# One transformer step with split products: token chunks 364/364/360 against 128 plain and 2 x 480 split

## The reference

```python
h = rms_norm(x, g0) * (1 + sc_a) + sh_a
proj = h @ w_in                       # 1024 -> 2432, then attention and the RWKV-7 scan
m = concatenate([o_attn, o_rw]) @ w_out
x = x + gt_a * rms_norm(m, g1)
h = rms_norm(x, g2) * (1 + sc_f) + sh_f
f = (silu(h @ w_gate) * (h @ w_up)) @ w_down     # 1024 -> 2816 -> 1024
x = x + gt_f * rms_norm(f, g3)
```

## Time and profile before

| | |
|---|---|
| Median of 3 runs | 2487.2 us (2483.46 to 2495.3) |
| The profiled execution | span 2496.6 us, 9.4 us above the median |
| TensorE matmul busy | 2098.6 us, 84% |
| VectorE busy | 940.9 us, 38% |
| ScalarE busy | 642.4 us, 26% |
| GpSimd busy | 202.4 us, 8% |
| DMA | 147.53 MB, 59 GB/s in the mean |

### The profile page before, as it was taken

The page is one execution under the profiler, slowest core; times in us unless marked ns, Lnnn a source line. Parts: engine busy times, 40 slices in busy tenths (PEclk is TensorE's granted clock), DMA queues, the critical chain, the costliest instruction groups (busy, mean ns, idle before and its releaser), DMA issues. The chain is left out here.

```text
span 2496.6 us, 38394 instructions
## 1 busy us (share of the span) xinstructions
PE 2098.6 (84%) x15782; PEld 1779.0 (71%) x15782; DVE 940.9 (38%) x1433; ACT 642.4 (26%) x1215; POOL 202.4 (8%) x283
## 2 busy tenths in 40 slices
PE   7499974199889889879867598499999999999985
PEld 2499952066667657656652297399999999999984
DVE  2211154445344434434521803623422333323336
ACT  2523342023323323323421412521111111111101
POOL 0000000032323212312300000100000000000000
PEclk9799996599999978989978799799999999999998
DMA  6011115701001001000019231211111011111022
GB/s 241 29 47 42 34 51 149 195 27 41 17 20 38 16 17 41 16 16 18 4 42 293 73 117 41 73 35 51 51 51 43 18 42 50 50 45 40 19 98 72
DMA packets 112112, 147.53 MB, mean 59 GB/s; under 512 B 65920, under 2 KB 80896, under 8 KB 111520
## 3 DMA queue, kind: packets, MB, share of 16 engines
q1 hardware_dynamic: 111968, 145.41, 18.0%
HBM read 114.90 MB, written 30.50 MB: 58 GB/s over the span
## 5 line engine op out<-in xcount | busy, mean ns | idle before, releaser
L1848 PE MATMUL ps<-hhi,whi 128*128 128x364 f32 (+1 forms) x1056 | 348.5, 330 | 33.1 <-DVE hlo L1087 27.9
L1848 PE MATMUL ps<-hlo,whi 128*128 128x364 f32 (+1 forms) x1056 | 348.4, 330 | 0.0
L1848 PE MATMUL ps<-hhi,wlo 128*128 128x364 f32 (+1 forms) x1056 | 348.3, 330 | 0.0
L347 DVE TENSOR_TENSOR wlo<-wraw,whi 128x1024 fp32r<-128x1024 f32 x72 | 88.0, 1225 | 525.3 <-ACT whi L343 525.3
L360 PE MATMUL ps<-hhi,whi 128*128 128x364 f32 (+1 forms) x672 | 222.7, 331 | 58.6 <-DVE hlo L1087 31.8
L1848 PEld LDWEIGHTS ps<-hhi,whi 128*128 128x128 f32 x1056 | 199.7, 189 | 34.2 <-DVE hlo L1087 28.5
L360 PE MATMUL ps<-hlo,whi 128*128 128x364 f32 (+1 forms) x672 | 222.5, 331 | 0.0
L360 PE MATMUL ps<-hhi,wlo 128*128 128x364 f32 (+1 forms) x672 | 222.3, 331 | 0.0
L1825 PE MATMUL ps<-ahi,dhi 128*128 128x364 f32 x528 | 180.8, 342 | 24.9 <-DVE acc L1427 16.8
L1848 PEld LDWEIGHTS ps<-hlo,whi 128*128 128x128 f32 x1056 | 199.6, 189 | 0.0
L1848 PEld LDWEIGHTS ps<-hhi,wlo 128*128 128x128 f32 x1056 | 199.6, 189 | 0.0
(11 more groups left out here) (204 smaller groups left out, 3133.1 us busy)
## 6 DMA issues: line engine op xcount, KB each, us to landing
wraw<-in_w_tiles SPq DMA_DIRECT2D x72, 512.0 KB, 3.4
late<-in_ada_w SPq DMA_DIRECT2D x8, 2048.0 KB, 8.1
ci<-scan SPq DMA_DIRECT2D x17, 768.0 KB, 4.5
draw<-in_w_down SPq DMA_DIRECT2D x22, 512.0 KB, 3.3
slab<-in_ada_w SPq DMA_DIRECT2D x4, 2048.0 KB, 18.2
scan<-mix SPq DMA_DIRECT2D x12, 512.0 KB, 4.4
x<-in_x_t SPq DMA_DIRECT2D x4, 1456.0 KB, 9.6
x<-x_mid SPq DMA_DIRECT2D x1, 4352.0 KB, 14.1
```

The costliest lines, as they stand in the source:

```text
L347: nc.vector.tensor_tensor(wlo[u][:, :, :], wraw[u][:, :, :], whi[u][:, :, :].bitcast(F32), ALU.subtract).then_inc(w_lo, 1)
L1848: mm = nc.tensor.matmul(ps[:, 3 * u + c, 0:n], w[u][:, k, :], x[:, k, a:a + n], start=(k == 0 and w is whi and x is hhi), stop=(k == KD - ...
```

## The change

CH becomes (960, 128), (0, 480), (480, 480). Chunk 0 (WHOLE) is multiplied in plain fp32 straight from unsplit operands: the loaded weights wraw, and hf, a copy of the input's last 128 tokens. Chunks 1 and 2 stay split. In the down pass chunk 0 multiplies draw by af, and draw has two buffers, loaded as a pair once the preceding down pass has ended. A weight load now also waits until the plain part of that buffer's last tile is done. The attention's q and k chunks keep 364/364/360 (QCH). All norms, residuals and stores that loop over CH take the new chunks. In the diff, renamed semaphore counts in GpSimd's, ScalarE's and VectorE's other waits are left out.

```diff
@@ -44,7 +44,10 @@
 NEG = -1e30
-CH = [(0, 364), (364, 364), (728, 360)]
+TF = 960
+CH = [(TF, T - TF), (0, 480), (480, 480)]
+WHOLE = 0
+QCH = [(0, 364), (364, 364), (728, 360)]
 CM = 363
...
@@ -161,11 +164,13 @@
         wraw, whi, wlo = [wraw0, wraw1], [whi0, whi1], [wlo0, wlo1]
-        hhi, hlo, R2 = place(R1, ("hhi", [P, KD, T], F32R), ("hlo", [P, KD, T], F32R))
+        hhi, hlo, hf, end = place(R1, ("hhi", [P, KD, TF], F32R), ("hlo", [P, KD, TF], F32R), ("hf", [P, KD, T - TF]))
+        R2 = R1 + 2 * KD * T * 4
+        assert end <= R2
         END = nc.sbuf_usable_end
-        sq = [P, 4, 364]
+        sq = [P, 4, 480]
         x1, s0, s1, r0, r1, end = place(R2, ("x1", [P, KD, T]), ("sq1_0", sq), ("sq1_1", sq), ("mrow0", [2, 512]), ("mrow1", [2, 512]))
@@ -230,11 +235,11 @@
         assert end <= END
-            R2, ("acc", [P, KD, T]), ("ahi", [P, 4, T], F32R), ("alo", [P, 4, T], F32R), ("draw", [P, D]),
+            R2, ("acc", [P, KD, T]), ("ahi", [P, 4, TF], F32R), ("alo", [P, 4, TF], F32R), ("af", [P, 4, T - TF]), ("draw0", [P, D]), ("draw1", [P, D]),
         assert end <= END
...
@@ -326,13 +331,14 @@
         def o_parts(h):
-            return [(h[:, 0:KR, :], oatt[:, :, :]), (h[:, KR:KD, :], yt[:, :, :])]
+            return [(h[:, 0:KR, :], oatt[:, :, 0:TF]), (h[:, KR:KD, :], yt[:, :, 0:TF])]
         def load_weight(eng, m, u, first=False):
                 eng.wait_ge(w_lo, 2 * m + u - 1)
+                eng.wait_ge(out_ready[u], 3 * m - 2)
             eng.dma_start(wraw[u][:, :, :].rearrange("p a b -> p (a b)"), d["w_tiles"][2 * m + u, :, :]).then_inc(w_in_sem[u], 16)
@@ -348,18 +354,31 @@
         def project(pe, m, u, first=False, tokens=None):
-            pe.wait_ge(w_lo, 2 * m + u + 1)
-            for c, (a, n) in enumerate(CH):
-                if tokens is not None:
-                    pe.wait_ge(lo_ready, tokens + c + 1)
+            for c in range(3):
+                if c == WHOLE:
+                    pe.wait_ge(w_in_sem[u], 16 * (m + 1))
+                    if tokens is not None:
+                        pe.wait_ge(hf_ready, tokens // 2 + 1)
+                else:
+                    pe.wait_ge(w_lo, 2 * m + u + 1)
+                    if tokens is not None:
+                        pe.wait_ge(lo_ready, tokens + c)
                 if not first:
                     pe.wait_ge(bank_free[u], 3 * (m - 1) + c + 1)
-                out = ps[:, 3 * u + c, 0:n]
-                for k in range(KD):
+                tile_products(u, c).then_inc(out_ready[u], 1)
+
+        def tile_products(u, c):
+
+            a, n = CH[c]
+            out = ps[:, 3 * u + c, 0:n]
+            for k in range(KD):
+                if c == WHOLE:
+                    mm = nc.tensor.matmul(out, wraw[u][:, k, :], hf[:, k, :], start=(k == 0), stop=(k == KD - 1))
+                else:
                     for w, x in ((whi, hhi), (whi, hlo), (wlo, hhi)):
                                               start=(k == 0 and w is whi and x is hhi), stop=(k == KD - 1 and w is wlo))
-                mm.then_inc(out_ready[u], 1)
+            return mm
         NORMS = {"n1": (KD, D), "q": (KQ, QL), "kv": (KKV, KVL), "m": (KD, D), "n2": (KD, D), "f": (KD, D)}
@@ -575,6 +594,7 @@
             sp.wait_ge(osplit_lo, 2)
+            sp.wait_ge(hf_ready, 2)
             for c, (a, n) in enumerate(CH):
@@ -587,21 +607,27 @@
             sp.wait_ge(sq_used, first_piece["n2"] + 6)
-            def load_down(g, u, first=False):
+            def load_down(g, first=False):
                 if not first:
-                    sp.wait_ge(d_lo, 2 * g + u)
-                sp.dma_start(draw[:, :], d["w_down"][bass.ds((2 * g + u) * P, P), :]).then_inc(d_in, 16)
+                    sp.wait_ge(d_lo, 2 * g)
+                    sp.wait_ge(down_ready, 24 * g + 1)
+                for u in range(2):
+                    sp.dma_start(draw[u][:, :], d["w_down"][bass.ds((2 * g + u) * P, P), :]).then_inc(d_in[u], 16)
             load_weight(sp, FF_M + 1, 0)
             load_weight(sp, FF_M + 1, 1)
-            load_down(0, 0, first=True)
-            with sp.Fori(1, GROUPS) as g:
-                for j in range(2):
-                    for u in range(2):
-                        load_weight(sp, 2 * g + FF_M + j, u)
-                load_down(g - 1, 1)
-                load_down(g, 0)
-            load_down(GROUPS - 1, 1)
+            load_down(0, first=True)
+            load_weight(sp, FF_M + 2, 0)
+            load_weight(sp, FF_M + 2, 1)
+            load_weight(sp, FF_M + 3, 0)
+            load_weight(sp, FF_M + 3, 1)
+            with sp.Fori(2, GROUPS) as g:
+                for u in range(2):
+                    load_weight(sp, 2 * g + FF_M, u)
+                load_down(g - 1)
+                for u in range(2):
+                    load_weight(sp, 2 * g + FF_M + 1, u)
+            load_down(GROUPS - 1)
             for u in range(2):
...
@@ -717,12 +744,17 @@
                 a, n = CH[c]
-                for k in range(KD):
-                    for b, w, s in segments(c):
-                        step.mark(nc.scalar.activation(src[:, k, b:b + w], src[:, k, b:b + w], ACT.Identity,
-                                                       bias=mod[:, shift + k, s:s + 1], scale=gains[:, gain, k, s:s + 1]))
-                step.wait()
-                nc.scalar.copy(hhi[:, :, a:a + n], src[:, :, a:a + n]).then_inc(hi_ready, 1)
+                parts = [(k, b, w, s) for k in range(KD) for b, w, s in segments(c)]
+                for i, (k, b, w, s) in enumerate(parts):
+                    dst = hf[:, k, b - TF:b - TF + w] if c == WHOLE else src[:, k, b:b + w]
+                    ins = nc.scalar.activation(dst, src[:, k, b:b + w], ACT.Identity, bias=mod[:, shift + k, s:s + 1], scale=gains[:, gain, k, s:s + 1])
+                    if c == WHOLE and i == len(parts) - 1:
+                        ins.then_inc(hf_ready, 1)
+                    else:
+                        step.mark(ins)
+                if c != WHOLE:
+                    step.wait()
+                    nc.scalar.copy(hhi[:, :, a:a + n], src[:, :, a:a + n]).then_inc(hi_ready, 1)
             act.wait_ge(gains_done, 1)
...
@@ -995,11 +1028,16 @@
             act.wait_ge(mod_done, SLABS)
-            for dst, src in o_parts(hhi):
+            for i, (dst, src) in enumerate(o_parts(hhi)):
                 nc.scalar.copy(dst, src).then_inc(osplit_hi, 1)
+                ins = nc.scalar.copy(hf[:, KR * i:KR * i + KR, :], (oatt, yt)[i][:, :, TF:T])
+                if i == 0:
+                    step.mark(ins)
+            ins.then_inc(hf_ready, 1)
             act.wait_ge(osplit_lo, 2)
+            act.wait_ge(hf_ready, 2)
             for n in range(KD):
@@ -1019,24 +1057,28 @@
             def down_hi(g, u):
-                act.wait_ge(d_in, 16 * (2 * g + u + 1))
+                act.wait_ge(d_in[u], 16 * (g + 1))
                 act.wait_ge(down_ready, 24 * g + 1)
-                nc.scalar.copy(dhi[u][:, :], draw[:, :]).then_inc(d_hi, 1)
+                nc.scalar.copy(dhi[u][:, :], draw[u][:, :]).then_inc(d_hi, 1)
             def gate(g, slot, j, first=False, last=False):
                 m = 2 * g + FF_M + j
-                q = 6 * g + 3 * j
+                q, q2 = 6 * g + 3 * j, 4 * g + 2 * j
                 for c, (a, n) in enumerate(CH):
                     if not (first and j == 0):
-                        act.wait_ge(act_lo, q + c - 2)
+                        if c == WHOLE:
+                            act.wait_ge(prod_ready, q - 2)
+                        else:
+                            act.wait_ge(act_lo, q2 + c - 2)
                     nc.scalar.activation(sil[c][:, 0:n], ps[:, c, 0:n], ACT.Silu).then_inc(sil_ready, 1)
                     act.wait_ge(down_ready, 24 * (g - 1) + 1)
-                for c, (a, n) in enumerate(CH):
+                for c in (1, 2):
+                    a, n = CH[c]
                     act.wait_ge(prod_ready, q + c + 1)
@@ -1083,7 +1125,7 @@
                 a, n = CH[c]
-                dve.wait_ge(hi_ready, count + 1)
+                dve.wait_ge(hi_ready, count)
                 nc.vector.tensor_tensor(hlo[:, :, a:a + n], src[:, :, a:a + n], hhi[:, :, a:a + n].bitcast(F32), ALU.subtract).then_inc(lo_ready, 1)
...
@@ -1395,26 +1437,30 @@
                 times_rstd(m1, x2, c)
-            for c in range(3):
-                rest(m1, c, 3 + c)
+            for c in (1, 2):
+                rest(m1, c, 2 + c)
             def down_lo(g, u):
                 dve.wait_ge(d_hi, 2 * g + u + 1)
-                nc.vector.tensor_tensor(dlo[u][:, :], draw[:, :], dhi[u][:, :].bitcast(F32), ALU.subtract).then_inc(d_lo, 1)
-
-            def product(g, slot, j, last=False):
+                nc.vector.tensor_tensor(dlo[u][:, :], draw[u][:, :], dhi[u][:, :].bitcast(F32), ALU.subtract).then_inc(d_lo, 1)
+
+            def product(g, slot, j, first=False, last=False):
                 m = 2 * g + FF_M + j
```

(73 more changed lines are left out.)

12 lines of the change are left out of this document (6 added, 6 removed).

## The result

The changed kernel takes 2532.8 us (median of 4 runs, 2525.06 to 2535.72); the kernel before took 2485.33 us beside it (4 runs, 2481.48 to 2495.3). The ratio is 1.0184, with a 95% interval of 1.0155 to 1.0213. So it is slower by 1.8%, 47.5 us, and 21 us above the top of the forecast range. The forecast was 2480 us; rival (d), a fixed cost of every fp32r product, gave 2535 us.

A forecast was written before the change was run, and what follows sets the result against it. The kernel was taken as bound by how fast TensorE starts products where weight tiles are streamed. Terms -32.0 + 28.6 - 3.6 = -7.0 us gave 2489.6 us profiled, 2480 us as median, range 2452 to 2512 us.

The forecast's parts named there:

- rival (d): Every fp32r product: the 0.0148 us above 0.152 us is a fixed cost; +55 us, 2535 us; chance 0.08.
- What a product costs: TensorE's fp32r products: starts are paced by a floor of 0.1665 us, so 480 columns cost 0.2025 us.
- Weight tiles: 72 streamed input, output and gate/up tiles: each saves 0.42 us, 30.2 us together; -32.0 us with the first tile's start.
- the change of form: Weight tiles: 0.06 us added per tile for two switches between plain and split products, bounds 0 and 0.2.
- Down passes: 11 feed-forward down passes: adder waits lengthen them, ten passes take 300.0 us, the last 28.4 us; together +28.6 us.
- The hold: Down passes: TensorE waits 0.45 us for the adder and restarts 0.10 us late, 0.56 us, seven times a pass.
- The start of a pass: Down passes: the adder comes after splits and remainders; TensorE resumes at 3.94 us, its wait grows to 2.3 us.
- The rest: Small terms at start, output product, norms, last store and last down loads: sum -3.6 us, bounds within 3 us each.
- What was costed at nothing: Weight loads waiting for the previous tile's plain part, paired down loads queued behind the preceding pass: no cost expected.
- (b): Down passes: the clock falls in seven short idle gaps a pass, 27 us in 11 passes, 2507 us; chance 0.20.
- (c): Down passes: the adder doesn't hold TensorE, 11 x 3.9 us less, 2437 us; chance 0.08.
- (e): Tiles and down passes: plain records are held to 0.1665 us like fp32r, about 2546 us; chance 0.04.

The follow-up runs named there:

- the streams: Two kernels with only back-to-back products by width, form, weight columns and start column, not the step; 480 fp32r columns took 0.2167 and 0.2175 us.
- the third experiment: Changed kernel with the 16 wide units of each down pass first and the 8 plain ones after: 2496.84 us, ratio 1.0046 to the kernel before.
- the first stream kernel: Computes nothing of the step, only streams of 96 products differing in width, form, weight columns and start column; 480 fp32r columns took 0.2167 us.
- the sixth experiment: Changed kernel with wide down units first and VectorE's remainders and weight split between the first additions: 2482.02 us, ratio 0.9994 to the kernel before.
- run 48: Not a follow-up run: "run" is the verb here, groups of four tiles run 48 products in 10.48 or 10.32 us; no measured kernel time belongs to it.

## Why the prediction was wrong

**The step that failed** is the one under "What a product costs": "So something else paces them, a floor of 0.1665 us", and from it "I take 0.2025 us" for 480 columns. It rested on two readings. The first, 360 columns no quicker than 364, was within the scatter of start columns (3 ns, where four columns are 1.7 ns). The second, no extra at half clock, is a sound row, but it doesn't exclude what I took it to exclude: the extra of about 0.015 us is there at 364 and at 480 columns alike and yet goes away at 1.2 GHz, as the after trace shows with 0.400 us for 480. Measured were 0.215 to 0.217 us for 480 columns, in the changed kernel and alone. Two points so close together can't tell a floor from a fixed cost, and I gave the fixed cost, rival (d), only 0.08.

**Weight tiles.** Forecast 11.56 us, measured 12.10 us. 48 products at 0.215 instead of 0.2025 us are +0.60 us; the 0.06 us for the change of form isn't there (10.32 + 1.78 us leaves nothing between), and 16 records at 0.1114 us are 1.78 us, as forecast. 72 x 0.54 = 39 us of the miss are here. The deeper mistake is the same one: with a fixed cost for each product, going from three chunks to two saves 24 x 0.015 = 0.36 us a tile, and the plain chunk costs 1.78 - 1.28 = 0.5 us more than its columns would in wide chunks. If part of the extra grows with the columns, as the streams suggest, both figures are smaller and their difference, 0.12 to 0.14 us, stays.

**Down passes.** The hold was forecast with its place, size and number: seven a pass of 0.56 us, "some 88 times, 40 to 60 us in total", and there were 85, 41.6 us, with the late restart on top. The start of a pass was right as well (wait 2.3 us forecast; the longest is 2.1). Summed over the chain, the ten passes took 306.5 us against 300.0 forecast, and the last one 31.5 against 28.4 us. The stretches of the first, second and fifth pass (columns as in the earlier trace rows; the granted clock is the third figure from the right):

```profile
1707.30:1739.00 31.70, 27.86 (x130) 23.20 (x130) 14.50 (x27) 1.54 (x2) 0.00 (x0) 0.95 0.00 1
1787.50:1818.00 30.50, 26.34 (x130) 22.00 (x129) 14.39 (x27) 1.54 (x2) 0.00 (x0) 1.00 0.00 1
...
2024.40:2056.00 31.60, 27.75 (x129) 23.17 (x128) 14.48 (x27) 1.54 (x2) 0.00 (x0) 0.95 0.00 0
```

At full clock the forecast was 29.3 us, and 96 wide products at 0.0135 us more make 30.6 us, which is what seven passes took. Two of the ten had a stretch at half clock, +1.1 us each, where I had counted 0.7 us for every pass; the tenth, with no weight split before it, took 29.1 us. The last pass is 1.3 us of the same and 1.8 us at its start: its first 6.0 us are at half clock, which costs 3.0 us where I had counted 1.5. One term of before was off too: the ten old passes took 270.4 us in the chain, not 273.4, since the tenth took 24.6 us. An addition of 480 columns, forecast at 0.65 us, took 0.65 to 0.67; the 3.19 us behind that forecast are VectorE's longest piece at L1087 (2912 columns), a row that the earlier trace rows doesn't show.

**The rest.** The small terms came to about what was forecast: the feed-forward part starts 1.6 us earlier (1607.7 against 1609.3 us), though the input tiles end 2.5 us later (338.1 against 335.6 us). What was costed at nothing did cost nothing: no wait for a weight load shows among TensorE's waits, and for the down loads only that before the last pass, 7.5 us where it was 8.1.

**Sum.** 39 us of tiles, 6.5 and 3.1 us of passes make 48.6 us; 2489.6 us was forecast for the profiled execution and its span was 2533.6 us, 44 us more, so some 5 us were better elsewhere. The forecast had taken over the old span with its two waits of 2.5 us behind down passes and the half clock behind one of them, 5.1 + 1.8 = 6.9 us; the changed kernel has neither, and no term of the forecast stood for that. The other 9 us of the miss of 52.8 us are the distance that I took over between execution and median; the profiled execution after lies 0.8 us above its median in span, and that before lay 9.4 us above.

**The rivals.** (b), a clock that falls in the idle gaps within a pass, didn't happen. The Trainium skill, "TensorE: Matmul & The Clock Gate", A second HAM failure mode, would have idling between groups of products, while PSUM banks are cycled through, make the clock swing. Here seven holds of about half a microsecond in each pass went by with the granted clock at 1.00, the level of 2.4 GHz; it fell in two of the ten, each time within 2 us behind the wait of 2 us at the start. (c) fell with the waits, (e) with the plain pace of 0.1115 us. (d) came true for 480 columns, in kind and in amount (that the extra isn't quite fixed in narrower products changes nothing here): it added 55 us, and by the measured paces it is 39 us in the tiles and 96 x 11 x 0.0135 = 14 us in the passes, 53 us. That its total of 2535 us lies so near to 2532.8 us is partly luck, since the offset between execution and median (+9 us) was made up by the clock in the passes and by what was better elsewhere.

Of the Trainium skill, "TensorE: Matmul & The Clock Gate", Back-to-back issue gap (columns/2.4 + 2.5 ns), the prediction had said that it disagrees at 364 columns and coincides with the sum at 480. The streams show that it holds for plain fp32 here, if both passes' columns are counted (0.4025 us for a record of two passes of 480 columns), and for fp32r at no width measured: 0.2280 us at 512 columns against 0.2158, and 0.2175 at 480 against 0.2025.

## What to carry to other kernels

Before a pace is extended to a width that the trace doesn't have, ask whether the rows can tell a floor from a fixed cost; two widths 1% apart can't, and a stream of products by themselves at three widths can. Fewer, wider chunks save what each product costs on top of its columns, here at most 0.36 us in a tile of 12 us; the narrow chunk that is left over then pays a whole weight load for each product, or two passes a record in plain form, and that was more. Where banks are used in turn, keep units equal: a short unit behind a long one leaves the long one's eviction uncovered, and what is moved out of the evictor's way at its first turn (here 18 us) can be worth more than the change of the products.

## What the runs showed of the hardware

- At full clock an fp32r product of 256 or more columns takes its columns at 2.4 GHz and 12 to 21 ns more, by width and start column (most 14 to 17); at 1.2 GHz nothing more (0.400 us for 480, 0.3025 us for 364 columns). With 480 columns it needs neither accumulation nor a change of weights, and it isn't shortened by 64 weight columns. With 64 weight columns it falls with the width, from 16.7 ns at 480 to 6.6 ns at 128 columns; how much of it belongs to the product and how much to the columns wasn't separated. What it is stays open.
- Plain fp32 took twice its columns at 2.4 GHz and 2 to 3 ns more for a record (0.4030 us for 480, 0.1625 for 192).
- With 128 weight columns no stream had a pace under 0.111 us at full clock, and none under 0.213 us at half clock. So for fp32r the width cost nothing up to 224 columns; with 64 weight columns 128 columns took 0.0599 us.
- A wait of 1.8 us at the start of a pass was followed by a stretch at half clock in eight of ten passes before, one of about 2 us in only two of ten after, and one of 1.5 to 1.6 us in none of nine in the third experiment. In the first stream kernel the clock fell to half for 17 us with no wait at all, in products of 64 columns started 0.111 us apart. Which falls where wasn't settled.
- In the third and the sixth experiment's kernels whole groups of four tiles run 48 products in 10.48 us and others in 10.32 us, at the same clock: 3 ns a product, the size of the scatter by start column. No run looked for its cause.
